# Stick-breaking attention beside a conformer convolution: a head's scores in three parts inside dense units, the value products of two heads alternating

## The reference, cut to what matters

```
h = RMSNorm(x); p = h @ w_in      # columns: GLU a | GLU b | q | k | v | gate_conv | gate_attn
glu = a * sigmoid(b);  conv = silu(LayerNorm(depthwise_conv_31(glu))) @ w_pw2
z = q.k / sqrt(64);  mask = k_pos < q_pos
log_1m = where(mask, log_sigmoid(-z), 0)
tail = reverse cumulative sum of log_1m over the keys, own key left out
attn = where(mask, exp(log_sigmoid(z) + tail), 0) @ v        # 16 heads of 64
x += (sigmoid(gate_conv) * conv + sigmoid(gate_attn) * attn) @ w_out
x += relu(RMSNorm(x) @ w_up)^2 @ w_down;  y = RMSNorm(x)
```

## Time and profile before

| what | value |
|---|---|
| median of 3 runs | 1073.31 us (1073.18 to 1075.3) |
| profiled execution, span from first to last instruction | 1073.2 us |
| the runs' fastest, beside that span | 1073.18 us |
| PE busy | 1050.9 us, 98% |
| PE's weight loads | 1001.3 us, 93% |
| DVE, ACT, POOL busy | 568.0, 462.7, 346.0 us |
| mean granted clock of PE | 0.965 |
| a turn of the loop | 61.4 us |
| moved by DMA | 83.55 MB, 78 GB/s |

### The profile page before, as it was taken

One profiled execution on the slowest core, in us unless ns is written; L12 is line 12 of the kernel. 1 busy time (PEld: TensorE's weight loads), 2 busy tenths in 40 slices (PEclk: granted clock), 3 DMA queues, 4 the chain that ended last, 5 costly groups with the idle time before them and its releaser, 6 DMA issues.

```text
span 1073.2 us, 19817 instructions
## 1 busy us (share of the span) xinstructions
PE 1050.9 (98%) x7761; PEld 1001.3 (93%) x7761; DVE 568.0 (53%) x821; ACT 462.7 (43%) x722; POOL 346.0 (32%) x171
## 2 busy tenths in 40 slices
PE   7999999999999999999999999999999999999996
PEld 6899898889998888899989999999999999999995
DVE  4349697878869787887986533222211112221122
ACT  4455454545555464545558333443411123341132
POOL 4412121322222122221152433434434324344230
PEclk8989898999989898998999999999999999999998
DMA  6221313222131223112331323232332223323102
GB/s 197 71 71 32 99 40 91 59 69 61 31 99 46 84 59 91 48 36 61 91 99 60 98 80 98 80 98 78 98 111 86 82 67 87 90 86 118 59 20 84
DMA packets 157745, 83.55 MB, mean 78 GB/s; under 512 B 3696, under 2 KB 156544, under 8 KB 157709
## 3 DMA queue, kind: packets, MB, share of 16 engines
q1 hardware_dynamic: 147261, 78.21, 25.0%
q10 hardware_dynamic: 10448, 4.84, 1.5%
HBM read 75.97 MB, written 7.06 MB: 77 GB/s over the span
## 4 chain that ended last, share of the span: by engine, by line
PE 94%; DVE 2%; SPq 1%; ACT 1%; DMA 1%; issue 0%; POOL 0%; ACTq 0%; DVEq 0%
PE dense L414 76%; PE z L500 4%; PE z L472 4%; PE pv L530 4%; PE z L467 2%; PE dense L538 1%; PE z L475 1%; DMA w_raw<-in_w_in_dram 1%; PE z L533 1%; DVE n L1048 1%; DVE sum_sq L1204 0%; SPq L297 0%; POOL r_lo L395 0%; DVE yconv L1199 0%; SPq L278 0%
## 5 line engine op out<-in xcount | busy, mean ns | idle before, releaser
L389 POOL TENSOR_TENSOR w_lo<-w_raw,w_hi 128x1024 fp32r<-128x1024 f32 x136 | 335.1, 2467 | 690.6 <-ACT w_hi L716 690.6
L414 PE MATMUL dense<-r_hi,w_hi 128*128 128x272 f32 (+1 forms) x1280 | 277.0, 298 | 2.4 <-DVE r_lo L1051 1.1
L414 PE MATMUL dense<-r_lo,w_hi 128*128 128x272 f32 (+1 forms) x1280 | 272.5, 295 | 0.0
L414 PE MATMUL dense<-r_hi,w_lo 128*128 128x272 f32 (+1 forms) x1280 | 272.0, 294 | 0.0
L1067 DVE SCALAR_TENSOR_TENSOR acc<-conv_in,cw_cur,acc 128x574 f32<-128x574 f32 x232 | 214.6, 978 | 0.0
L414 PEld LDWEIGHTS dense<-r_hi,w_hi 128*128 128x128 f32 x1280 | 208.1, 195 | 3.4 <-issue 1.3
L414 PEld LDWEIGHTS dense<-r_hi,w_lo 128*128 128x128 f32 x1280 | 208.3, 194 | 0.0
L414 PEld LDWEIGHTS dense<-r_lo,w_hi 128*128 128x128 f32 x1280 | 207.9, 194 | 0.0
L716 ACT ACTIVATE w_hi<-w_raw 128x1024 fp32r<-128x1024 f32 x136 | 142.5, 1051 | 147.9 <-PE dense L414 132.9
L414 PE MATMUL dense<-s_hi,w_hi 128*128 128x272 f32 x640 | 132.6, 288 | 0.0
L414 PE MATMUL dense<-s_lo,w_hi 128*128 128x272 f32 x640 | 132.5, 288 | 0.0
(11 more groups left out here) (225 smaller groups left out, 1258.2 us busy)
## 6 DMA issues: line engine op xcount, KB each, us to landing
w_raw<-in_w_in_dram SPq DMA_DIRECT2D x56, 512.0 KB, 3.8
w_raw<-in_w_up_dram SPq DMA_DIRECT2D x32, 512.0 KB, 4.0
w_raw<-in_w_down_dram SPq DMA_DIRECT2D x32, 512.0 KB, 3.4
w_raw<-in_w_pw_dram SPq DMA_DIRECT2D x8, 512.0 KB, 3.5
w_raw<-in_w_out_dram SPq DMA_DIRECT2D x8, 512.0 KB, 3.4
out_dram<-v_tok ACTq DMA_DIRECT2D x8, 256.0 KB, 2.3
out_dram<-k_tok ACTq DMA_DIRECT2D x8, 256.0 KB, 2.3
out_dram<-y_tok SPq DMA_DIRECT2D x4, 512.0 KB, 3.9
```

Source lines behind the costliest of these rows:

```text
L389: pool.tensor_tensor(w_lo[:, s], w_raw[:, s], w_hi[:, s].bitcast(F32), ALU.subtract).then_inc(lo_done, 1)
L414: mm = nc.tensor.matmul(dense[:, slot, h, 0:half], w[:, wslot, k, :], m[:, k, c0 + h * half:c0 + (h + 1) * half], start=(k == 0 and n == 0 ...
```

## The change

The scores of a head become three functions, and a dense unit can call a function ahead of a chunk. The second head's scores move from the end of turn i into unit 0 of turn i+1, ahead of chunks 0, 3 and 6; the first head's third and second part and the transposes of v move into unit 3, ahead of chunks 4 and 2, while its first part stays ahead of the unit. The value products of both heads of a pair are made once a turn, behind unit 2 of the next turn, head by head in alternation. For this the two heads' logs and probabilities live in two buffers: what was `ez` and `sp` for every head is now `sp` for the first head's logs and probabilities and `ez` for the second's, with the sum written in place. `pv_done` rises once a turn instead of twice. DVE's and ACT's order of work is not changed.

```
-            def dense_unit(wslot, slot, m_hi, m_lo, c0, half, chunk_ready=None):
+            def dense_unit(wslot, slot, m_hi, m_lo, c0, half, chunk_ready=None, between=None):
                 for k in range(KC):
+                    if between is not None and k in between:
+                        between[k]()
...
-            def values(i, hh, first=False):
...
-                pe.wait_ge(prob_done, 3 * head + 3)
+            def values(i, first=False):
+                both = [(slice(hh * HD, (hh + 1) * HD), heads2[hh]) for hh in range(2)]
...
+                pe.wait_ge(prob_done, 3 * (2 * i + 1) + 3)
                 for n, (bank, off, cols, q0) in enumerate(KT):
-                    nc.tensor.matmul(pv[r, q0:SEQ], v_tok[:, n, r], prob[:, bank, off:off + cols], start=(n == 0), stop=False, skip_group_check=True)
+                    for r, prob in both:
+                        nc.tensor.matmul(pv[r, q0:SEQ], v_tok[:, n, r], prob[:, bank, off:off + cols], start=(n == 0), stop=False, skip_group_check=True)
...
                     pe.wait_ge(gb_log, i)
-                    unit(0, 0, True)
+                    part = scores(prev, 1)
+                    unit(0, 0, True, between={0: part[0], 3: part[1], 6: part[2]})
...
                 unit(2, 1)
                 if not first:
-                    values(prev, 1)
-                scores(i, 0, first)
-                if not first:
-                    pe.wait_ge(ktok_kept, i)
+                    values(prev)
+                part = scores(i, 0, first)
+
+                def values_back():
+                    if not first:
+                        pe.wait_ge(ktok_kept, i)
+                    turn_back(vT, 0).then_inc(tile_done, 1)
+
+                def last_part():
+                    part[2]()
+                    values_back()
+                part[0]()
                 pe.wait_ge(v_kept, i + 1)
-                turn_back(vT, 0).then_inc(tile_done, 1)
-                unit(3, 1)
+                unit(3, 1, between={2: part[1], 4: last_part})
...
                 unit(5, 1, True)
-                values(i, 0, first)
-                scores(i, 1)
+                pe.wait_ge(prob_done, 6 * i + 3)
...
-                    nc.vector.scalar_tensor_tensor(sp[:, b, 0:c], z[:, b, 0:c], 0.0, ez[:, b, 0:c], ALU.max, ALU.add).then_inc(sp_done, 1)
+                    nc.vector.scalar_tensor_tensor(sp[:, b, 0:c], z[:, b, 0:c], 0.0, sp[:, b, 0:c], ALU.max, ALU.add).then_inc(sp_done, 1)
```

More of the change, by code:

```diff
@@ L475, in mask, with tile_0, tiles_2_3, tile_1 @@
                     return nc.tensor.matmul(z[:, bank, off:off + m.shape[1]], ident_b[:], m, start=False, stop=False, skip_group_check=True)
[L477 to L492, removed]
+                def tile_0():
+                    if hh == 0:
+                        pe.wait_ge(ckT_kept, i + 1)
+                        pe.wait_ge(q_kept, i + 1)
+                        pe.wait_ge(k_kept, i + 1)
+                    score(*S_CACHE0, ckT[r, 0:P], SEQ, OUTTOK, start=True)
+                    score(*S_CACHE1, ckT[r, P:2 * P], SEQ, OUTTOK)
+                    score_split(0, 0, 0, 0, start=True)
+                    mask(0, 0, neg_diag[:, META:P]).then_inc(z_scored, 1)
+                def tiles_2_3():
+                    for j in (2, 3):
+                        bank, off, _, q0 = KT[j]
+                        score_split(bank, off, j, q0)
+                        mm = mask(bank, off, neg_diag[:])
+                    mm.then_inc(z_scored, 1)
+                def tile_1():
+                    if hh == 0 and not first:
+                        pe.wait_ge(mix_s_done, i)
+                    bank, off, _, q0 = KT[1]
+                    score_split(bank, off, 1, q0, start=True)
+                    mask(bank, off, neg_diag[:])
+                    score(*LAST, kT[r, 4 * P:5 * P], SEQ - META, OUTTOK)
+                    mask(*LAST, neg_last[:]).then_inc(z_scored, 1)
+                return tile_0, tiles_2_3, tile_1
             def cumulate(head):
@@ L625, in gate_conv @@
                     claim(f % 2, X_EMPTIED[f % 2] + f // 2)
-                dense_unit(f % RING, f % 2, r_hi, r_lo, META, HALFO)
+                dense_unit(f % RING, f % 2, r_hi, r_lo, META, HALFO, between=between)
             pe.wait_ge(gb_log, KC)
-            gate_conv(0)
+            part = scores(KC - 1, 1)
+            gate_conv(0, between={0: part[0], 3: part[1], 6: part[2]})
             pe.wait_ge(ga_log, KC)
@@ L637, in _ @@
             gate_conv(2)
-            values(KC - 1, 1)
+            values(KC - 1)
             gate_conv(3)
@@ L765, in log_sigmoid_parts, with softplus_logs @@
                 nc.scalar.activation(dst, dst, ACT.Ln, bias=1.0).then_inc(s_ln, 1)
-            def softplus_logs(head, between=None):
+            def softplus_logs(head, hh, between=None):
+                ez = heads2[hh]
                 def a(n):
@@ L796, in softplus_logs, with probabilities @@
                     step(n)
-            def probabilities(head):
+            def probabilities(head, hh):
+                prob = heads2[hh]
                 act.wait_ge(cum_done, head + 1)
@@ L912, in _ @@
             keys_out(KC - 1, FIRST_POST + 2, 0)
-            probabilities(2 * KC - 1)
+            probabilities(2 * KC - 1, 1)
             high_post(0, 1)
@@ L1110, in turn, with tile_sums @@
                 o3 = KT[3][1]
-                def tile_sums(head):
+                def tile_sums(head, hh):
+                    sp = heads2[hh]
                     dve.wait_ge(sp_done, 3 * head + 3)
```

63 lines of the change are left out of this document (30 added, 33 removed).

## The result

The changed kernel takes 1099.79 us (median of 4 runs, 1099.09 to 1100.6), the kernel before 1073.63 us in the same comparison (4 runs, 1073.18 to 1075.3). The ratio is 1.0242, with a 95% interval of 1.0227 to 1.0257: slower by 26.2 us. The forecast was 1092 us, 1076 to 1112.

A forecast was written before the change was run, and what follows sets the result against it. PE bounds the kernel before; after the change DVE's round would, at 64.2 us a turn against 61.4. From 1073.2: six turns +16.8, first turn -2.9, last turn and way out +5, giving 1092 us, range 1076 to 1112.

The forecast's parts named there:

- Sign and cause: Slower by 1.7%: DVE's round outlasts PE's own 56.6 us turn, so PE waits about 6.1 us at key transposes and unit 2.
- (a) The low stretch behind the scores: PE's half-clock stretch at the scores' end, transposes and dense pairs disappears, saving 2.95 us in each of 8 turns.
- (b) Values: Both heads' alternating value products on PE overlap and take 3.1 us, between bounds 2.82 and 5.64, saving 2.5 per turn.
- Switches: Cutting scores between dense blocks on PE adds two returns per head, 0.35 us each head, 0.7 per turn.
- The round: Serial steps from one keys kept to the next, mostly over DVE: 60.7 us, 62.7 with the subtraction meeting.
- The meeting at the three taps: POOL's second subtraction falls on DVE's three taps before k_lo and adds 2.0 us to the round.
- the clock: PE's new waits bring a 3.4 us half-clock stretch in unit 2, adding 1.5 us: 64.2 us a turn.
- last turn and way out: PE's savings, switches, wait for keys and a later convolution mean behind the loop: +5 us in all.
- 1 (PE's own work stays the bound): Rival: round below 56.6 us, kernel faster, 1036 us; chance 0.14 with all that is over 0.2% faster.
- 2 (no overlap): Rival: alternating value products on PE do not overlap, values cost 5.64 us, total 1110 us; chance 0.26.
- 3: Rival: PE's waits do not lower the clock, 7 x 1.5 us less, total 1081 us; chance 0.12.
- 4: Rival: POOL's second subtraction meets no tap and the clock holds, 1069 to 1075 us; chance 0.04 for no change.

The follow-up runs named there:

- experiment 1: Changed kernel with seven of DVE's convolution taps moved earlier (three between q_lo and k_lo, four in and behind head 0's softplus): 1051.77 us.
- experiment 2: Kernel before the change, with the same seven convolution taps moved as in experiment 1: 1073.45 us, ratio 0.9993.
- experiment 11: Changed kernel with the taps moved as in experiment 1 and both heads' scores in one piece: 1051.76 us.
- experiment 10: Changed kernel with the taps moved as in experiment 1 and the parts of the scores closer together (ahead of blocks 0, 1 and 3): 1033.14 us.
- experiment 4: Changed kernel with both heads' scores in one piece again, values still alternating: 1059.31 us.
- experiment 5: Changed kernel with head 0's scores alone in one piece ahead of unit 3, head 1's still in parts: 1105.36 us.
- experiment 6: Changed kernel with head 1's scores alone in one piece ahead of unit 0, head 0's still in parts: 1093.21 us.
- experiment 7: Changed kernel with only the two taps behind head 0's sums_low moved ahead of its softplus sums: 1099.39 us.
- experiment 3: Changed kernel with the value products of a pair issued head by head instead of alternating: 1115.55 us.
- experiment 9: Kernel before the change, with head 0's scores alone in three parts inside unit 3, values as before: 1086.03 us.

## Why the prediction was right, point by point

- **Sign and cause: right.** PE's own turn was forecast at 56.6 and DVE's round as longer; PE was to wait at the key transposes and at unit 2. It waits there, 1.7 and 3.8 us, for `q_lo` and for the copies into `kT`: 5.5 together, forecast 6.1. A third wait, 0.7 us for head 0's probabilities ahead of head 1's scores, was not forecast. Experiments 1 and 2 show that DVE's order, worth nothing before, now sets the time, and experiment 11 against 10 that PE's gain on the clock was real.
- **(a) The low stretch behind the scores, 2.95 a turn: gone, as counted.** Experiment 11 puts it at 3.0 (most turns take 58.6 us, against the 55.6 of the undisturbed turn in experiment 4, both with undivided scores).
- **(b) Values, 3.1 taken: 2.82.** The lower bound, which I had not dared to take. By the Trainium skill (TensorE: Matmul & The Clock Gate, "Part 3: Packing small matmuls") 3.6 us was the estimate; its factor is for three narrower column tiles, and the trace of two 64-column halves shows no loss against one head alone.
- **Switches, 0.7 a turn: too dear.** The turn of 55.6 us in experiment 4 and the 55.85 of experiment 10 have neither wait nor low clock, and differ by the four extra changes and returns: about 0.25 a turn, 0.06 each. The Trainium skill (TensorEngine Tiling (Array Packing), "Key Properties") says that changing the tiling mode drains the engine. These turns bound the price of it here; they do not show the drain apart from other small differences.
- **The round, 62.7 without the clock.** By its steps, forecast and measured: unit 2 with the gap 6.34 + 1.5 for the clock, 8.59; values 3.1, 2.82; parts of the scores 7.76, 7.53 (244.82 to 252.35); to the first sum 1.62, 1.62; sums to `sums_low` 7.15, 7.16; two taps to the copies 5.74, 7.68 (261.13 to 268.81); `gate_b` 1.51, 1.46; from there to the keys 29.44 with the meeting, 28.00. Together 64.2 and 64.86.
- **The meeting at the three taps: right** (6.37, forecast 4.28 + 2.0). What I missed is that POOL's other subtractions move against DVE as well: the two taps behind `sums_low` now take 3.68, not 1.54, and the gated product 0.71, not 2.45. These two nearly cancel. I had moved one subtraction and should have moved all of a turn.
- **The steps that were mis-sized most are two of DVE's**: two taps to the copies, 1.9 too short, and from the gated product to the keys, 1.4 too long. That they nearly cancel is luck. **Of the terms that do not cancel, the clock is the largest**: +1.5 for 3.4 us at half speed, whereas the low stretch is 6.8 us long and covers most of unit 2, which takes 2.1 us more. The turn is 64.9 instead of 64.2. Six turns gave 21.2 instead of 16.8, the first -3.4 instead of -2.9, last turn and way out +6.8 instead of +5, and the start of the loop comes 0.6 later: 25.2 in spans instead of 18.9. For the way out the prediction named the mean of the convolution (L643 before); PE shows no wait for it there, but one of 3.2 us for POOL's `w_lo`, with 3.4 us at half clock.
- **What the sum did not contain**: the round has a second branch, over PE's units 3, 4, 5, 0 and head 1's last mask, as long as the one I added up (experiments 5, 6 and 7). That it did not harm this forecast is luck too, since the two are 0.1 us apart; a forecast of any single repair by my chain alone was wrong, as my expectations for experiments 5 and 6 were.
- **Rivals.** 1 (PE's own work stays the bound) is what experiment 10 makes true by moving taps and parts. 2 (no overlap) was put at 1110 and measured at 1115.6 in experiment 3. 3 and 4 did not occur: all seven waits at unit 2 go with a low stretch, and the second subtraction meets the taps each time.
- One statement ahead of the prediction needs a correction. Device time and span do not agree within 0.1 us: in each of the runs above the device time is 1.7 us over its own span. By the same difference the span of 1073.2 belongs to an execution of about 1074.9 us. The forecast, made as a difference to that span, is not touched by more than this.

## What to carry to other kernels

An engine that is busy 98% hides how near the next chain is. Before its work is shortened, add up the serial round through the other engines, and every branch of it: with two equal branches a repair of one measures as little or nothing, and what pays is a repair of both or of what lies behind their meeting. Here, cutting the scores delayed a mask on which the slower chain hung; moving three vector taps out of that chain turned a loss of 26 us into a gain of 15, and seven taps and closer parts turned it into a gain of 40.

## What the runs showed of the hardware

- Value products of the two column halves of PE, issued in turns, run beside one another in full: starts 0.01 us apart, 2.82 us for both against 5.31 head by head. Issued head by head only the seam overlaps, 0.33 us (5.64 - 5.31).
- A wait of PE of 1.71 us with transposes behind it left the clock up (experiment 1), waits of 2.7 and 3.8 us went with a fall (experiment 4 and the changed kernel), and so did two short ones close together, 1.3 and 0.9 us, at the start of the loop (the changed kernel; the same place in the kernel before is in the earlier trace rows). Undivided scores lowered it in some turns and not in others of the same kernel (experiment 4), so turns of one kernel take 55.6 or 58.6 us by it alone; a claim on the clock wants the trace of every turn.
- A vector operation with both inputs in SBUF waits out a POOL subtraction that it meets: two taps 1.54 and 3.68 us beside none and one of them, three taps 2.26, 4.39 and 6.37 us beside none, one and two. In experiments 4 and 9 PE waited at unit 2 in just the turns ahead of which three taps had met two.
